# A decoder step with 64 experts on one core: high and low parts of the 64 sample tokens packed side by side in the gate units

## What is computed

```
x2 = h.reshape(n * s, D_MODEL)
eidx, gw = route(x2, w_router, router_bias)          # 6 of 64 experts for each token
ffn = swiglu(x2, w_s_gate, w_s_up, w_s_down) + routed_experts(x2, eidx, gw, w_e_gate, w_e_up, w_e_down)
ple = sigmoid(h @ w_ple_gate) * (p @ w_ple_proj)
h = layer_norm(DN_ALPHA * h + ffn + ple, ln2_g, ln2_b)
```

## Time and profile before

| | us |
|---|---|
| median of 3 runs | 1254.81 |
| the three runs | 1254.39, 1254.81, 1257.17 |
| the profiled execution, own time | 1258.23 |
| its span (first to last instruction) | 1256.3 |
| PE busy | 1217.8 (97% of the span) |
| PE weight loads busy | 963.5 (77%) |
| DVE busy | 514.2 (41%) |
| ACT busy | 318.5 (25%) |
| POOL busy | 159.4 (13%) |

### The profile page before, as it was taken

The page is one execution under the profiler, slowest core; times in us unless marked ns, Lnnn a source line. Parts: engine busy times, 40 slices in busy tenths (PEclk is TensorE's granted clock), DMA queues, the critical chain, the costliest instruction groups (busy, mean ns, idle before and its releaser), DMA issues.

```text
span 1256.3 us, 23679 instructions
## 1 busy us (share of the span) xinstructions
PE 1217.8 (97%) x8816; PEld 963.5 (77%) x8817; DVE 514.2 (41%) x1165; ACT 318.5 (25%) x614; POOL 159.4 (13%) x227
## 2 busy tenths in 40 slices
PE   8999999999999999999899999989999999999887
PEld 8999978999999999998899565555555555556543
DVE  4666773432444323576885212111222222111137
ACT  4364653322212222316012111111111111111121
POOL 0200000000000000004236112111121121221200
PEclk9999999999999999999999999999999999999999
DMA  8212223223232232605427999999999999999987
GB/s 265 85 56 68 68 51 69 68 67 101 68 93 75 71 116 67 212 22 208 172 96 306 420 419 420 420 421 419 420 421 420 420 419 418 420 422 421 421 363 296
DMA packets 98657, 307.31 MB, mean 245 GB/s; under 512 B 11245, under 2 KB 62405, under 8 KB 72841
## 3 DMA queue, kind: packets, MB, share of 16 engines
q1 hardware_dynamic: 85332, 275.20, 56.5%
q0 software_dynamic: 12304, 28.60, 5.9%
q10 hardware_dynamic: 948, 2.50, 0.5%
HBM read 294.45 MB, written 26.94 MB: 256 GB/s over the span
## 4 chain that ended last, share of the span: by engine, by line
PE 50%; DMA 42%; DVE 5%; issue 1%; DVEq 1%; ACT 0%; SPq 0%; POOL 0%; ACTq 0%; POOLq 0%
DMA w_exp<-in_w_e_down_dram 40%; PE proj L1073 32%; PE proj L1283 4%; PE proj L1424 3%; PE att L1205 1%; PE att L1167 1%; PE att L1292 1%; PE proj L1107 1%; DMA fold<-expert_rows 1%; PE proj L1378 1%; PE att L1218 1%; PE proj L1408 1%; DVE res L2182 1%; PE att L1283 1%; DMA expert_rows<-ysb,sidx_col 1%
## 5 line engine op out<-in xcount | busy, mean ns | idle before, releaser
L1494 PE MATMUL att<-w_exp,xt 128*64 128x256 f32 x2560 | 286.6, 380 | 10.5 <-DMA w_exp<-in_w_e_up_dram 8.1
L1494 PEld LDWEIGHTS att<-w_exp,xt 128*64 128x64 f32 x2560 | 191.2, 137 | 115.4 <-issue 38.3
L1073 PE MATMUL proj<-h_hi,w_hi 128*128 128x288 f32 x768 | 168.2, 301 | 0.3 <-DVE w_lo L474 0.3
L1073 PE MATMUL proj<-h_hi,w_lo 128*128 128x288 f32 x768 | 164.4, 296 | 0.0
L1073 PE MATMUL proj<-h_lo,w_hi 128*128 128x288 f32 x768 | 164.3, 296 | 0.0
L1514 PE MATMUL proj<-w_exp,ht_e 128*64 128x512 f32 x640 | 146.2, 598 | 4.2 <-DMA w_exp<-in_w_e_down_dram 4.2
L1073 PEld LDWEIGHTS proj<-h_hi,w_hi 128*128 128x128 f32 x768 | 122.6, 189 | 6.1 <-issue 4.6
L1073 PEld LDWEIGHTS proj<-h_lo,w_hi 128*128 128x128 f32 x768 | 123.8, 189 | 0.0
L1073 PEld LDWEIGHTS proj<-h_hi,w_lo 128*128 128x128 f32 x768 | 123.6, 189 | 0.0
L474 DVE TENSOR_TENSOR w_lo<-w_raw,w_hi 128x2048 fp32r<-128x2048 f32 x33 | 75.6, 2291 | 93.2 <-ACT w_hi L464 88.5
L1514 PEld LDWEIGHTS proj<-w_exp,ht_e 128*64 128x64 f32 x640 | 44.0, 137 | 76.5 <-issue 72.5
(11 more groups left out here) (392 smaller groups left out, 1873.2 us busy)
## 6 DMA issues: line engine op xcount, KB each, us to landing
w_exp<-in_w_e_gate_dram SPq DMA_DIRECT2D x64, 1024.0 KB, 16.8
w_exp<-in_w_e_up_dram SPq DMA_DIRECT2D x64, 1024.0 KB, 17.0
w_exp<-in_w_e_down_dram SPq DMA_DIRECT2D x64, 1024.0 KB, 17.0
w_raw<-in_w_in_dram SPq DMA_DIRECT2D x21, 1024.0 KB
part<-expert_rows SPq DMA_DIRECT2D x8, 1536.0 KB, 20.5
w_raw<-in_w_in_dram SPq DMA_DIRECT2D x8, 512.0 KB
w_raw<-in_w_attn_out_dram SPq DMA_DIRECT2D x8, 512.0 KB
w_raw<-in_w_conv_out_dram SPq DMA_DIRECT2D x4, 1024.0 KB
```

Of the source, the lines that this page charges most:

```text
L1073: last = nc.tensor.matmul(proj[:, 2 * i + a, 0:HALF], lhs, x[:, c, a * HALF:(a + 1) * HALF], start=(c == 0 and n == 0), stop=(c == KC - 1 ...
L1494: last = nc.tensor.matmul(att[e * SLOT:(e + 1) * SLOT, m, 0:FF], xt[:, c, e * SLOT:(e + 1) * SLOT], weights[e][:, c, :], start=(c == 0), s ...
```

## The change

The transposed 64 sample tokens are copied once into `xt_both`, for each piece of the contraction 64 columns of high parts and beside them 64 columns of low parts. A unit of the 64-token tile is then 8 pieces by two products, `[x_hi | x_lo]` by `w_hi` and by `w_lo`: 16 products instead of 24. The upper half of the bank holds the rows of the low parts. VectorE adds the halves (`packed_add`: a copy of the upper half into `sig_g`, then an add), and ScalarE takes the sigmoid of the sum from `sig_g`. The term of low by low is now included. Unit 19 is done whole at the head of the last block's high half, and no longer in its low half.

```diff
+        xt_both = at("xt_both", [P, KC, 2, NS], F32R, o_x + 36864)
...
+        packed_sum, PACKED_0 = s_sub, 1
...
-            sp.wait_ge(u_ready, N_BLK * NT)
+            sp.wait_ge(u_ready, N_BLK * NT - 1)
...
+            act.drain()
+            nc.scalar.activation(xt_both[:, :, 0, :], xt_hi[:, :, SEQ:T].bitcast(F32), ACT.Copy)
+            act.wait_ge(x2_lo, 2 * NT)
+            nc.scalar.activation(xt_both[:, :, 1, :], xt_lo[:, :, SEQ:T].bitcast(F32), ACT.Copy)
+            act.drain()
             act.wait_ge(lt_mm, 1)
...
             def gate_sigmoid(u):
 
                 w = ntok(u % NT)
+                if u % NT == NT - 1:
+                    act.wait_ge(packed_sum, PACKED_0 + u // NT + 1)
+                    nc.scalar.activation(sig_g[0:w, u % NSIG, :], sig_g[0:w, u % NSIG, :], ACT.Sigmoid).then_inc(u_sig, 1)
+                    return
...
+            def packed_unit(u, whi, wlo):
+
+                for c in range(KC):
+                    both = xt_both[:, c, :, :].rearrange("p a n -> p (a n)")
+                    for n, v in enumerate((whi, wlo)):
+                        last = nc.tensor.matmul(gate_bank(u), both, v[:, c, :],
+                                                start=(c == 0 and n == 0), stop=(c == KC - 1 and n == 1))
+                return last
...
+                if t == NT - 1:
+                    last = packed_unit(u, whi, wlo)
...
+                if high:
+                    pe.wait_ge(u_sig, N_BLK * NT - 6)
+                    packed_unit(N_BLK * NT - 1, whi, wlo)
+                for t in range(NT - 1):
...
+            def packed_add(u):
+
+                if u == N_BLK * NT - 1:
+                    dve.wait_ge(tb_used, NTK // TPAIR + 1)
+                else:
+                    dve.wait_ge(u_ready, u + 1)
+                dve.wait_ge(u_mul, u - NSIG + 1)
+                o, total = gate_bank(u), sig_g[0:NS, u % NSIG, :]
+                nc.vector.tensor_copy(total, o[NS:P, :])
+                dve.drain()
+                nc.vector.tensor_tensor(total, total, o[0:NS, :], ALU.add).then_inc(packed_sum, 1)
+
             for m in range(NTK // TPAIR):
...
+                if m in (4, 9):
+                    packed_add(m)
...
             for u in range(2 * NT, 3 * NT):
+                if u == 3 * NT - 2:
+                    packed_add(3 * NT - 1)
                 ppo_add(u)
+            packed_add(N_BLK * NT - 1)
             xt_half(0)
```

More of the change, by code:

```diff
@@ L998, in gate_sigmoid @@
                     act.wait_ge(u_mul, u - NSIG + 1)
-                nc.scalar.activation(sig_g[0:w, u % NSIG, :], gate_bank(u)[0:w, :], ACT.Sigmoid).then_inc(u_sig, 1)
+                nc.scalar.activation(sig_g[0:w, u % NSIG, :], gate_bank(u), ACT.Sigmoid).then_inc(u_sig, 1)
             for u in range(N_BLK * NT):
@@ L1411, in table_products @@
                 last.then_inc(tb_used, 1)
+            def packed_unit(u, whi, wlo):
[5 more added lines that the diff above has]
+                return last
             def gate_unit(u):
                 j, t = u // NT, u % NT
-                w = ntok(t)
                 if t == 0:
@@ L1421, in gate_unit @@
                     pe.wait_ge(u_sig, u - 1)
[L1422 to L1425, removed]
+                if t == NT - 1:
+                    last = packed_unit(u, whi, wlo)
+                else:
+                    for c in range(KC):
+                        for n, (x, v) in enumerate(((xt_hi, whi), (xt_hi, wlo), (xt_lo, whi))):
+                            last = nc.tensor.matmul(gate_bank(u), x[:, c, t * P:(t + 1) * P], v[:, c, :],
+                                                    start=(c == 0 and n == 0), stop=(c == KC - 1 and n == 2))
                 last.then_inc(u_ready, 1)
@@ L1441, in last_block @@
                 terms = ((xt_hi, whi), (xt_hi, wlo)) if high else ((xt_lo, whi),)
-                for t in range(NT):
-                    u, w = 3 * NT + t, ntok(t)
+                if high:
+                    pe.wait_ge(u_sig, N_BLK * NT - 6)
+                    packed_unit(N_BLK * NT - 1, whi, wlo)
+                for t in range(NT - 1):
+                    u = 3 * NT + t
                     if high and t == 3:
@@ L1447, in last_block @@
                         for n, (x, v) in enumerate(terms):
-                            last = nc.tensor.matmul(gate_bank(u)[0:w, :], x[:, c, t * P:t * P + w], v[:, c, :],
+                            last = nc.tensor.matmul(gate_bank(u), x[:, c, t * P:(t + 1) * P], v[:, c, :],
                                                     start=(high and c == 0 and n == 0), stop=(not high and c == KC - 1))
```

## The result

The changed kernel is slower: 1259.99 us median (1257.77 to 1262.85, 5 runs) against 1254.81 (1253.90 to 1257.17, 5 runs). The ratio is 1.0034, 95% interval [1.0024, 1.0045]. The forecast was 1255.3 us with a range of 1253.4 to 1258.0 and 0.82 on no change: wrong, on the slow side. The profiled execution of after took 1257.77 us (span 1255.9), the lowest of its five. It is 0.5 us less than the profiled one of before, so the two traces can't be subtracted: where the loss sits has to be read from stretches of them.

What follows compares the result with a forecast made beforehand. Expert weight transfers were taken as the bound, so only the stream's start and holes count: +0.2 (routed later) +0.9 (hole) -0.65 (dip gone) = +0.45 us on 1254.81, giving 1255.3 us, range 1253.4 to 1258.0.

Steps and rivals of the forecast that it cites:

- What bounds the kernel: Expert phase: transfer-bound at about 420 GB/s; only the weight stream's start and its holes move the end.
- TensorE's own work: Packed units: 16 products take 1.91 us, saving 0.83 to 0.89 us per unit.
- Places A and B: Units 4 and 9: units 6 and 11 wait for VectorE's adds, 0.8 and 1.1 us; routed 0.2 us later.
- Rival 3: Clock falls in the gaps before units 6 and 11, some 1.8 us longer each, 1258.9 us; chance 0.04.
- Place C: Unit 14, before the weight parts at hs_hd: packed add behind VectorE's queue makes hs_hd 1.95 us later, at 677.6.
- rival 2: Unit 14's packed add stretched next to POOL: hs_hd at 679.5, hole grows, 1257.2 us; chance 0.13.
- The hole: Weight stream runs dry near 678 us, before the parts issued at hs_hd arrive: 0.9 us lost.
- The dip of before: Low transfer rate before 683 us in the kernel before, expected to go: 0.65 us gained.
- Place D: First expert pair: starts about 688.4 instead of 687.2 behind unit 19's add; covered by the transfer-bound phase, otherwise 1.2 us.
- ScalarE's two copies: Copies into xt_both, some 0.6 us each, fall into 3.94 us of ScalarE idleness before lt.

Runs made afterwards that it cites:

- e4_c: Changed kernel with ScalarE's copy hs_x moved ahead of unit 14's sigmoid: 1259.30 us, ratio 1.0023 to the kernel before.
- e9_before: Kernel before, unchanged, run again as a control and for a second trace: 1256.03 us, ratio 1.0001.
- e1_same: Changed kernel run again unaltered: 1261.23 us, ratio 1.0042 to the kernel before.
- e10_same: Changed kernel run a third time unaltered: 1259.66 us, ratio 1.0030 to the kernel before.
- e3_d: Changed kernel with the copy of xt's second half put ahead of adding unit 19's halves: 1260.03 us, ratio 1.0031 to the kernel before.

## Why the prediction was wrong, point by point

**What bounds the kernel** held in the main: the stream is fed by landings before and after, and the places named were the right ones. That "the end is fixed by bytes", so that each hole counts in full, is not what e4_c's trace shows.

**TensorE's own work** held: units 14 and 19 together are 32 products in 3.84 us, 1.92 each against 1.91 forecast.

**Places A and B: the step that failed.** "The whole saving of unit 4 goes into a wait of 0.8 us" and "routed comes 0.2 us later". In place of the +0.2, RS grew by 2.2 us (the first trace of after against e9_before) or by 2.8 (e1_same against the trace that I read, with a fall of the clock in it). The chain was right in form and nearly in size: from the start of m = 9's last table operation to unit 11 it took 659.22 - 657.33 = 1.89 us, against 1.7 forecast. What it was laid beside was wrong, in two ways. First, "in the changed kernel some tenths sooner; I take 658.4": that is 32.56 us behind the first tables' products, and it came at 32.86. VectorE gained 0.25 us there and nothing in e1_same (33.12 against 33.11 before), since its queue had become the chain. In an execution of the kind that I read, unit 11 then comes at 35.0 (e1_same, e4_c, e10_same) against 34.04, so about the bound "0.9 us later if m = 9 isn't sooner at all", not the +0.2 taken. Second, the times of before were taken from one profiled execution as the kernel's. Its 6 us at the low clock delayed TensorE and so gave VectorE waits of 0.70 and 1.48 us, which looked like slack. In e9_before TensorE is 1.2 us sooner and that slack is 0.62 us. There the two added operations and the sigmoid all land on the path: unit 11 at 34.75 against 32.79, 2.0 us later, and the restart behind the wait adds 0.3 (3.13 against 2.86 us for the unit). RS is 40.31 against 38.08.

**Rival 3, the clock, had 0.04 and happened at one of its two gaps.** "The gaps at A and B are 0.8 and 1.1 us, so I don't expect it." The gap at B was 1.86 us, and behind it the clock fell in e1_same, e4_c and e10_same, but not in the first trace of after or in e3_d (1.85 us). Each such trace has RS 42.1 instead of 40.3 to 40.5; 1.5 us of it lie between unit 11 and routed (7.07 or 7.08 against 5.56), near the 1.8 that the rival named. The fall at unit 6 never came (0.8 to 1.8 us). The Trainium skill (TensorE: Matmul & The Clock Gate, section "HAM oscillation — how this bites in real kernels") warns of long idle gaps. The fall behind the 3.41 us wait agrees with it; these runs add that falls also come behind a wait of 1.86 us, in some executions.

**Place C** held in its chain. That the issue at hs_hd was forecast for 677.6 and came at 677.68 is luck: counted from the first tables' products it is 51.8 us forecast and 53.2 measured. The parts: add of unit 12 until 675.2, copy 0.43, add 0.41, sigmoid 0.42, hs_x 1.15. VectorE's rows there and at unit 19:

```profile
675.24 0.43 DVE L2074 COPY sig_g<-proj 64x256 f32<-64x256 f32 x1
675.74 0.41 DVE L2076 TENSOR_TENSOR sig_g<-sig_g,proj 64x256 f32<-64x256 f32 x1
...
685.89 0.43 DVE L2074 COPY sig_g<-proj 64x256 f32<-64x256 f32 x1 [8.02 <-POOL ppo L707]
```

The stretch that rival 2 needed didn't come. At 675.24 POOL was idle (its product ended at 674.95), so that place says nothing on it; at 685.89 the copy ran wholly beside

```profile
683.66 2.83 POOL L707 TENSOR_TENSOR ppo<-ppo,sig_g 128x256 f32<-128x256 f32 x4
```

and took the same 0.43 us, while a table operation with both inputs in SBUF took 1.53 us at 639.51 beside a product of POOL. By the Trainium skill (SBUF — State Buffer, section "SBUF: two separate sides") GpSimd holds up a VectorE operation only with two SBUF inputs or in a two-port mode. The trace agrees with both: 1.53 us for the first, 0.43 for the copy from PSUM. The hole was put at 0.9 us and was 1.6, because the distance from routed to hs_hd was 12.9 us (664.78 to 677.68) and not the 12.2 forecast (665.4 to 677.6). The dip of before (0.65 us) went, as forecast. Net +0.9 instead of +0.25 in bytes; E shows +0.82 against e9_before and nothing against the other trace of before, and e4_c's E doesn't fall when the hole goes, so in time this term lies between nothing and that.

**Place D** held: covered (e3_d). ScalarE's two copies cost nothing: the first tables' products start at 624.27 to 624.47 in three traces of the changed kernel, 624.42 in e9_before.

**What the sum leaves open.** Three traces of the changed kernel have spans of 1255.9, 1257.5 and 1257.7 (mean 1257.0), two of before 1256.3 and 1252.8 (1254.6): 2.5 us, of which RS is 2.8, E 0.4 and the start -0.7. The medians differ by 0.35%, 4.4 us. The profiled executions of the changed kernel were the fastest of their runs in two of three cases; what the others have more of was not traced. More falls of the clock are not most of it: the mean granted clock is on record for each execution. Beside e10_same it is 0.9947 in the changed kernel (7 executions) and 0.9944 in the kernel before (23), and the loss is 3.4 us all the same; in e1_same it is 0.9932 against 0.9946. Between executions of the kernel before, 0.001 of mean clock goes with 0.4 to 0.5 us, so by this estimate falls, wherever they lie, are none of the loss in one case and some 0.7 us of 4.6 in the other. The rest of the gap between traces and medians stays open.

## What to carry to other kernels

Read more than one execution before you call an engine's idle time slack: a stretch at a low clock on the bounding engine lends waits to every other engine, and in the next execution they are gone. Before moving work to an engine whose queue feeds the bound, measure where that queue ends (here 33.3 to 33.6 us behind the first tables' products) against the other engine's arrival (32.8 to 34.0), and with the added work put at each place in it: in the rearranged kernels it ended at 32.8 to 35.5. Shorter work on the bounding engine is worth nothing beyond the point where it meets that queue.

## What the hardware showed that was not expected

- After the same 3.41 us wait the stretch at the 1.2 GHz level (granted clock 0.50) took away 1.7 us of full clock in some executions and 3.4 in others, in both kernels: the trace read for the prediction has 3.4, e9_before 1.7, the first trace of after 1.7, e1_same 3.4.
- The clock fell behind a wait of 1.86 us in three of five traces that had one (with 1.85 to 1.86), for 1.5 us of TensorE's time each. In those three the stretch behind the 3.41 us wait had been the long one; in the other two, the short one. Why is open.
- Behind the 2.3 us wait at the first pair it also fell in some traces and not in others (0.66 against 1.00 over 688 to 693).
- A fall near 175 us, far ahead of the change, is in the first trace of before and not in e9_before; everything behind it is shifted by about 1.4 us (625.84 against 624.42). Five further traces have it, and in them the first tables' products start at 625.87 to 626.23; without it, at 624.27 to 624.63.
